# Expert stage of a Trainium2 kernel: token rows in blocks of 116 and 148 columns, the lower product turned round

## The reference, cut to what matters

```python
def moe_swiglu(t, w_router, w1, w3, w2):
    logits = (t @ w_router).astype(jnp.float32)
    top_v, top_i = lax.top_k(logits, TOP_K)                 # TOP_K = 2
    gates = jax.nn.softmax(top_v, axis=-1).astype(t.dtype)
    e_flat = top_i.reshape(-1)
    order = jnp.argsort(e_flat)
    tok = order // TOP_K
    xs = t[tok]
    sizes = jnp.bincount(e_flat, length=N_EXPERTS).astype(jnp.int32)
    h = jax.nn.silu(lax.ragged_dot(xs, w1, sizes)) * lax.ragged_dot(xs, w3, sizes)
    y = lax.ragged_dot(h, w2, sizes) * gates.reshape(-1)[order][:, None]
    return jnp.zeros_like(t).at[tok].add(y)
```

## Time and profile before

| | |
|---|---|
| median of 3 runs | 10121.22 us (10114.34 to 10128.42) |
| profiled execution: its time | 10121.75 us |
| profiled execution: its span | 10120.1 us |
| granted TensorE clock, mean | 0.969 |
| TensorE busy | 9577.1 us, 95% of the span |
| matmuls of the upper products, line 2387 | 3722.5 us busy, 32256 instructions |
| matmuls of the lower product, line 2397 | 1814.6 us busy, 4032 instructions |
| expert stage: its first DMA is issued at 4469.7 us, the next stage's at 10022.3 us | 5552.6 us |

### The profile page before, as it was taken

How to read it: one execution, slowest core, us unless ns; L and a number is a source line. 1 busy time by engine, 2 the same in 40 slices (tenths; PEclk the granted TensorE clock), 3 DMA queues, 4 the chain that set the end, 5 groups by cost and what they waited for, 6 DMA issues and landing times. The chain is left out here.

```text
span 10120.1 us, 132287 instructions
## 1 busy us (share of the span) xinstructions
PE 9577.1 (95%) x51446; PEld 6599.4 (65%) x51447; DVE 2676.1 (26%) x5608; ACT 1214.8 (12%) x3139; POOL 339.4 (3%) x524
## 2 busy tenths in 40 slices
PE   9974999999999998989999999999999999999995
PEld 3444577644444443458788788878788788788784
DVE  1137444332223224531111111111111111111113
ACT  1123233220000002220100100000100100100001
POOL 0010000012000000010000000000000000000002
PEclk9986999999999999989999999999999999999997
DMA  5312000149200002232211211122211211211224
GB/s 201 122 51 87 3 5 5 66 178 387 83 19 19 25 19 69 99 123 100 92 62 62 73 50 50 50 83 74 82 59 53 83 50 62 78 55 62 79 100 178
DMA packets 435311, 809.45 MB, mean 80 GB/s; under 512 B 24220, under 2 KB 304844, under 8 KB 428192
## 3 DMA queue, kind: packets, MB, share of 16 engines
q1 hardware_dynamic: 370598, 562.48, 16.2%
q0 software_dynamic: 59040, 224.13, 5.6%
q10 hardware_dynamic: 5472, 19.93, 0.6%
HBM read 573.91 MB, written 232.54 MB: 80 GB/s over the span
## 5 line engine op out<-in xcount | busy, mean ns | idle before, releaser
L2387 PEld LDWEIGHTS ex_psH<-ex_xt,ex_w 128*128 128x128 f32 x32256 | 3698.5, 193 | 381.0 <-issue 381.0
L2387 PE MATMUL ex_psH<-ex_xt,ex_w 128*128 x32256 | 3722.5, 277 | 100.7 <-issue 77.6
L2397 PE MATMUL ex_psY<-ex_w,ex_a 128*128 128x512 f32 x4032 | 1814.6, 593 | 6.1 <-DVE ex_a L2511 6.1
L2511 DVE TENSOR_TENSOR ex_a<-ex_s,ex_psH 128x128 f32<-128x128 f32 x1008 | 290.3, 288 | 4532.6 <-PE ex_psY L2397 3263.3
L550 PE MATMUL de_ps<-de_ht,de_w 128*128 128x512 f32 x2816 | 1222.9, 592 | 0.0
L2397 PEld LDWEIGHTS ex_psY<-ex_w,ex_a 128*128 128x128 f32 x4032 | 727.6, 191 | 730.6 <-issue 730.6
L550 PEld LDWEIGHTS de_ps<-de_ht,de_w 128*128 128x128 f32 x2816 | 535.1, 190 | 672.3 <-issue 672.3
L2476 ACT ACTIVATE ex_s<-ex_psH 128x128 f32<-128x128 f32 x1008 | 279.3, 277 | 5046.6 <-PE ex_psH L2387 5046.6
L566 PE MATMUL de_ps<-de_w,de_a 128*128 128x512 f32 x1408 | 621.9, 594 | 18.0 <-DVE hx_h L716 18.0
L2521 DVE TENSOR_TENSOR ex_ya<-ex_psY,ex_ya 128x512 f32 x936 | 603.1, 685 | 25.4 <-PE ex_psY L2397 25.4
L231 PE MATMUL en_psO<-en_w,en_ht 128*128 128x512 f32 (+1 forms) x1152 | 501.1, 592 | 2.0 <-ACT en_ht L273 2.0
(11 more groups left out here) (329 smaller groups left out, 4526.9 us busy)
## 6 DMA issues: line engine op xcount, KB each, us to landing
ex_w<-in_o_w SPq DMA_DIRECT2D x336, 1024.0 KB, 7.7
xs<-de_zero POOLq DMA_DIRECT2D x130, 512.0 KB, 32.9
ys<-de_zero POOLq DMA_DIRECT2D x130, 512.0 KB, 33.1
en_ch<-in_w_mod SPq DMA_DIRECT2D x48, 1024.0 KB, 5.0
de_w<-in_e_w SPq DMA_DIRECT2D x66, 512.0 KB, 5.8
ex_x<-xs ACTq DMA_DIRECT2D x38, 512.0 KB, 3.6
ys<-ex_ya POOLq DMA_DIRECT2D x36, 512.0 KB, 9.4
proj<-en_o POOLq DMA_DIRECT2D x18, 1008.0 KB, 4.1
```

What stands on the lines that cost most here:

```text
L2387: last = nc.tensor.matmul(psH[:, h, q * P:(q + 1) * P], W[:, s, k, h * P:(h + 1) * P], XT[:, k, bass.ds(at, P)], start=k == 0, stop=k == K ...
L2397: last = nc.tensor.matmul(psY[:, c], A[:, h], W2[:, s, h, c * BANK:(c + 1) * BANK], start=h == 0, stop=h == HU - 1)
L2511: nc.vector.tensor_tensor(A[:, h], S[:, h], psH[:, h, P:2 * P], ALU.mult).then_inc(a_done, 1)
```

## The change

The rows of an expert are cut into blocks of two widths, `SLIM` = 116 and `WIDE` = 148 columns. With N rows there are nt = max(2, ceil((N + 32) / 148)) blocks, of which ceil((N - 116 nt) / 32), at least one, are wide. `CT` now holds for each expert the slim and the wide blocks, their sum, the number of 128-row tiles that they touch, and the two running sums; `TI` is gone.

The lower product is turned round: a 128x128 piece of `W2` is the held weight, and the block's 116 or 148 columns of `A` move; its 8 output pieces lie in three PSUM banks (`PARTS`) and `YA` now holds results with the feature on the partition. A block is therefore 64 + 32 instructions of the block's width. `down` follows in the same block: three first products need only half 0 of `A`, then TensorE waits for half 1. The silu writes `A`, and VectorE multiplies in place. The `drain` stands at the end of each chunk.

Token rows are loaded by SP straight into `XT`, all tiles of an expert after the last W3 product of the expert before. Then each tile is turned in place: VectorE and ScalarE copy it into a fixed buffer `T` in four quarters, TensorE turns each quarter (2 transposes), and VectorE and ScalarE bring it back to `XT`. After the last chunk every tile of `YA` goes through `T` and back in the same way before POOL stores it. POOL clears `YA` once at the start.

```diff
+            N, MT, LEFT = (NX[:, q] for q in range(3))
             settle(nc.vector.scalar_tensor_tensor(N, IO[0:1, :], -float(SEQ), psA[0:1, 1, 0:NE], ALU.mult, ALU.add))
+            settle(nc.vector.tensor_tensor(MORE[:, :, :], N.rearrange("p (e j) -> p e j", j=1).to_broadcast([1, NE, STEPS]),
+                                           AT_LEAST[:, :, :].to_broadcast([1, NE, STEPS]), ALU.is_ge))
+            settle(nc.vector.tensor_reduce(MT, MORE[:, :, :], AXX, ALU.add))
+            settle(nc.vector.scalar_tensor_tensor(LEFT, MT, -float(SLIM), N, ALU.mult, ALU.add))
+            settle(nc.vector.tensor_scalar(NI[:, :], LEFT, float(STEP - 1 - 2 * SLIM), float(STEP), ALU.add, ALU.max))
+            nc.vector.tensor_scalar(LAY[:, 2], MT, 2.0, None, ALU.add)
+            settle(nc.vector.tensor_scalar(NI[:, :], NI[:, :], STEP.bit_length() - 1, None, ALU.logical_shift_right))
+            nc.vector.tensor_scalar(LEFT, LAY[:, 2], float(SLIM), float(P - 1), ALU.mult, ALU.add)
+            settle(nc.vector.tensor_scalar(LAY[:, 1], NI[:, :], 0.0, None, ALU.add))
+            nc.vector.tensor_tensor(LAY[:, 0], LAY[:, 2], LAY[:, 1], ALU.subtract)
+            settle(nc.vector.scalar_tensor_tensor(NI[:, :], LAY[:, 1], float(STEP), LEFT, ALU.mult, ALU.add))
             settle(nc.vector.tensor_scalar(NI[:, :], NI[:, :], 7, None, ALU.logical_shift_right))
+            nc.vector.memset(LAY[:, 4:6, 0:1], 0.0)
+            settle(nc.vector.tensor_scalar(LAY[:, 3], NI[:, :], 0.0, None, ALU.add))
             for e in range(1, NE):
+                settle(nc.vector.tensor_tensor(LAY[:, 4:6, e:e + 1], LAY[:, 4:6, e - 1:e], LAY[:, 2:4, e - 1:e], ALU.add))
+            nc.vector.tensor_copy(CT[:, :, :], LAY[:, :, :])
...
+MAXB = 64
+SLIM, WIDE, STEPS = 116, 148, 13
+STEP = WIDE - SLIM
...
+        A = m.sbuf("a", [P, HU, WIDE])
+        T = m.sbuf("t", [P, KD, P])
         psH = m.psum("psH", [P, HU, BANK])
+        psY = m.psum("psY", [P, 3, BANK])
+        psT = m.psum("psT", [P, 3, BANK])
+        turns = [psT[:, 0], psT[:, 1], psT[:, 2], psH[:, 1]]
...
+            def weights(e, i, s):
+                f = i * 2 + s
+                at = [bass.ds(v, 1) for v in (e, f)]
+                sp.wait_ge(w_used, e * FC + f + 1)
+                sp.sem_inc(passed_sp, 1)
+                sp.dma_start(W1[:, s], w1v[at[0], at[1]].rearrange("a b p k n -> p (a b k) n")).then_inc(w_in[s], 16)
+                sp.dma_start(W3[:, s], w3v[at[0], at[1]].rearrange("a b p k n -> p (a b k) n")).then_inc(w_in[s], 16)
+                sp.dma_start(W2[:, s], w2v[at[0], at[1]].rearrange("a b p h n -> p (a b h) n")).then_inc(w_in[s], 16)
+
+            def token_rows(e):
+                nd, t0 = count(sp, 3, e, 3, NT + 1), count(sp, 4, e, 0, MAXB)
+                sp.wait_ge(gate_done, t0 * (FC * HU) + 1)
+                sp.sem_inc(passed_sp, 1)
+                with sp.Fori(0, nd) as d:
+                    row = (d + e * NT).with_bounds(min_val=0, max_val=NE * NT)
+                    sp.dma_start(XT[:, :, bass.ds(d * P, P)], rows(xs_d, row).rearrange("p (k n) -> p k n", n=P)).then_inc(x_in, 16)
+
+            def rest(e):
+                weights(e, 0, 1)
+                with sp.Fori(1, FC // 2) as i:
                     for s in range(2):
+                        weights(e, i, s)
+
+            sp.dma_start(ident[:, :], ident_d).then_inc(const_in, 16)
+            sp.dma_start(mod[:, :, :], cols).then_inc(const_in, 16)
+            token_rows(0)
+            weights(0, 0, 0)
+            rest(0)
+            with sp.Fori(1, NE) as e:
+                weights(e, 0, 0)
+                token_rows(e)
+                rest(e)
...
+            pool.memset(YA[:, :, :], 0.0).then_inc(y_free, 1)
+            with pool.Fori(0, NE) as e:
+                nd, d0 = tiles(pool, e)
+                with pool.Fori(0, nd) as d:
+                    for q in range(NQ):
+                        pool.wait_ge(t_out[q], d0 * 2 + nd + d + 2)
+                    row = (e * NT + d).with_bounds(min_val=0, max_val=NE * NT)
+                    pool.dma_start(rows(ys_d, row).rearrange("p (k n) -> p k n", n=P), YA[:, :, bass.ds(d * P, P)]).then_inc(stored, 16)
+                pool.wait_ge(stored, (d0 + nd) * 16)
...
+            def experts_block(width, at, s, n):
+                for h in range(HU):
+                    for q, W in enumerate((W1, W3)):
+                        pe.wait_ge((s_done, a_done)[q], n * HU + h + 1)
+                        for k in range(KD):
+                            last = nc.tensor.matmul(psH[:, q, h * width:(h + 1) * width], W[:, s, k, h * P:(h + 1) * P],
+                                                    XT[:, k, bass.ds(at, width)], start=k == 0, stop=k == KD - 1)
+                        last.then_inc((up_done, gate_done)[q], 1)
+
+                def down(r, k, h):
+                    j = k - PARTS[r][0]
+                    return nc.tensor.matmul(psY[:, r, j * width:(j + 1) * width], W2[:, s, h, k * P:(k + 1) * P], A[:, h, 0:width],
+                                            start=h == 0, stop=h == HU - 1)
+                pe.wait_ge(a_done, n * HU + 2)
+                for r, (lo, hi) in enumerate(PARTS):
+                    pe.wait_ge(y_added, n * 3 + r + 1)
+                    down(r, lo, 0)
+                pe.wait_ge(a_done, n * HU + 3)
+                for r, (lo, hi) in enumerate(PARTS):
+                    down(r, lo, 1)
+                for r, (lo, hi) in enumerate(PARTS):
+                    for k in range(lo + 1, hi):
+                        for h in range(HU):
+                            last = down(r, k, h)
                     last.then_inc(y_done, 1)
...
+            def turn(n):
+                for q in range(NQ):
+                    pe.wait_ge(t_in[q], n + 1)
+                    pe.wait_ge(t_out[q], n + 1)
+                    for j in range(2):
+                        last = nc.tensor.transpose(turns[q][:, j * P:(j + 1) * P], T[:, 2 * q + j], ident[:, :])
+                    last.then_inc(t_done[q], 1)
...
+                with pe.Fori(0, nd) as d:
+                    turn(d0 * 2 + d)
+                for q in range(NQ):
+                    pe.wait_ge(t_out[q], d0 * 2 + nd + 1)
+                pe.sem_inc(passed_pe, 1)
+                with pe.Fori(0, FC // 2) as i:
+                    for s in range(2):
+                        lo = pe.snap(t0 * FC + (na + nb) * (i * 2 + s), min_val=0, max_val=MAXB * FC)
+                        pe.wait_ge(w_in[s], (e * (FC // 2) + i + 1) * 48)
+                        pe.sem_inc(passed_pe, 1)
+                        with pe.Fori(0, na) as j:
+                            experts_block(SLIM, pe.snap((j * SLIM).with_bounds(min_val=0, max_val=XW - SLIM)), s, lo + j)
+                        with pe.Fori(0, nb) as j:
+                            experts_block(WIDE, pe.snap((na * SLIM + j * WIDE).with_bounds(min_val=0, max_val=XW - WIDE)), s, lo + na + j)
                         nc.tensor.drain().then_inc(w_used, 1)
...
+                with pe.Fori(0, nd) as d:
+                    turn(d0 * 2 + nd + d)
...
+            def silu(width, n):
+                for h in range(HU):
+                    act.wait_ge(up_done, n * HU + h + 1)
+                    nc.scalar.activation(A[:, h, 0:width], psH[:, 0, h * width:(h + 1) * width], ACT.Silu).then_inc(s_done, 1)
+
+            def fill(src, at, n):
+                act.wait_ge(t_done[1], n + 1)
                 act.sem_inc(passed_act, 1)
+                nc.scalar.activation(T[:, 2:4], src[:, 2:4, bass.ds(at, P)], ACT.Copy).then_inc(t_in[1], 1)
...
+                    act.wait_ge(x_in, (d0 + nd) * 16)
+                    fill(XT, at, d0 * 2 + d)
+                    for q in (1, 3):
+                        act.wait_ge(t_done[q], d0 * 2 + d + 2)
+                        act.sem_inc(passed_act, 1)
+                        for j in range(2):
+                            k = 2 * q + j
+                            last = nc.scalar.activation(XT[:, k, bass.ds(at, P)], turns[q][:, j * P:(j + 1) * P], ACT.Identity,
+                                                        bias=mod[:, 0, k:k + 1], scale=mod[:, 1, k:k + 1])
+                        last.then_inc(t_out[q], 1)
...
+            def gather(width, at, n, fresh, e):
+                for h in range(HU):
+                    dve.wait_ge(s_done, n * HU + h + 2)
+                    dve.wait_ge(gate_done, n * HU + h + 2)
+                    nc.vector.tensor_tensor(A[:, h, 0:width], A[:, h, 0:width], psH[:, 1, h * width:(h + 1) * width], ALU.mult).then_inc(a_done, 1)
+                if fresh:
+                    dve.wait_ge(y_free, e + 1)
+                for r, (lo, hi) in enumerate(PARTS):
+                    dve.wait_ge(y_done, n * 3 + r + 1)
+                    out = YA[:, lo:hi, bass.ds(at, width)]
+                    y = psY[:, r, 0:(hi - lo) * width].rearrange("p (k n) -> p k n", n=width)
+                    if fresh:
```

(45 more changed lines are left out.)

260 lines of the change are left out of this document (79 added, 181 removed).

## The result

The changed kernel takes 10300.41 us (median of 4 runs, 10290.29 to 10306.15), the kernel before 10117.78 us beside it (10109.70 to 10128.42): ratio 1.018, interval 1.0168 to 1.0191. It is slower by 183 us; the forecast was 127 us slower. The profiled execution has a span of 10300.3 us and a mean granted TensorE clock of 0.959, for 0.969 before.

A forecast was written before the change was run, and what follows sets the result against it. The expert stage was taken as bound by TensorE's instructions times their pace, plus small gaps. Blocks -92, chunk ends +85, turning +188, between experts -52 and routing -2 gave +127 us on 10121.75: 10248 us, range 10120 to 10350.

The forecast's parts named there:

- end: After the last expert: 0.8 us for the last adds and 9 for the last store and barrier, 10 us.
- The blocks: Expert stage's products: slim steps 0.1117 us, wide 0.1259, so 5240 us for 5332, 92 us less.
- Rival 1: Slim block steps go by columns, 0.0993 us each, saving 298 us more: 9950 us; chance 0.07.
- The wait inside a block: TensorE's wait for half 1 of A is covered by 0.07 to 0.11 us; priced at nothing.
- Rival 4: The wait for half 1 of A shows by 0.2 us in 462 blocks, 92 us: 10340 us; chance 0.07.
- The chunk ends: Drain at each chunk's end exposes sequencer work, about 1.35 us, 104 times: 140 us for 55, 85 more.
- Rival 3: Inner loop's branch pays for its length, 48 x 3.8 = 182 us at chunk ends: 10430 us; chance 0.07.
- Turning: Tiles through T: XT 3.3 us, YA 2.8, 36 each way, 220 us where 32 go away: +188.
- Rival 2: Turning and chunk ends are cheap, at their low bounds: -17 us, 10104 us; chance 0.09.
- Between experts: Seven boundaries, 8.3 us each beside turning, 58 us; with start and end 81 for 133: -52.
- Start: First expert, beside turning: three tiles land at about 10.3 us, then 1.0 and 2.0: 13.3 us.
- The routing chain: Before the expert stage: nine dependent operations fewer, 1 to 3 us, taken as 2 us less.

The follow-up runs named there:

- run 4: Changed kernel with SLIM and WIDE at 132 and 164 instead of 116 and 148: 10080.24 us, ratio to the kernel before 0.9956.
- run 5: Changed kernel without the drain at chunk ends, SyncE waiting on y_done before reloading a weight slot: 10157.66 us, 143 us less.
- run 6: Kernel before the change with its drains removed, SyncE waiting on y_done instead: 10076.03 us, ratio 0.9960.
- run 1: Changed kernel with one Copy activation on a scratch column ahead of the loop that turns the XT tiles: 10263.04 us, 37 us less.

## Why the prediction was right or wrong

The direction, the mechanism and the range (10120 to 10350) held; the likeliest time, 10248, was 52 us low. Against the stage of 5731.3 us the steps miss by 40 (boundaries), 6 (block phases), some 7 (start) and -2 (end); the stage itself begins 2.3 us later, where 2 us earlier were forecast.

- **The blocks, -92: right.** Slim steps are 0.112 us, wide ones 0.126; with the chunk ends and eight starts at half clock 5240 + 140 + 16 = 5396 us were forecast, 5402.5 measured. Rival 1 (columns) is refuted by 128, 116, 100 and 64 columns at 7.31 us for 64 instructions, and by run 4, in which more columns are faster. What is shown is the pace; that the load of the weight sets it is argued, since no run has the same instructions without their loads.
- **The wait inside a block, nothing: right.** No idle time stands before the lower product. The step from the seventh to the eighth lower product of a slim block is 0.133 us for 0.112, 0.02 x 252 = 5 us. Rival 4 is out.
- **The chunk ends, 140 for 55: right.** 139 now, by run 5; of the 55 before, run 6 gave back 40 with longer waits at the boundaries. Rival 3 is out. These are the sequencer's branches of the inner loop (line 2443) and of the loop over experts (line 2435); the shortest of each are the loops' ends:

```profile
L2443 PEldq COMPARE_BRANCH  x56: 73/216/216, 4570.0 to 10187.8; - x56
...
L2435 PEldq COMPARE_BRANCH  x8: 83/214/214, 4996.4 to 10194.5; - x8
```

  The first, over 768 instructions, takes the 0.21 us of the old one over 576; with its register work it makes 0.56 us at 48 ends, 27 us, not 182. The second takes 0.21 us too, for 4.0 before, as the forecast took it. The Trainium skill's rule that rival 3 named ("Runtime: NRT & Kernel Launch", "Instruction fetch mechanics"), with pages of 256 instructions, would have put a stall at each branch back over 768 instructions; the 216 ns of that row disagree. The same section of the Trainium skill also gives TensorE room for 2048 instructions, and with that the 4.0 us over some 1800 disagree.
- **Turning, +188: the step that failed, in size.** The sentence "ScalarE's own chain: copy 0.4, wait 0.9, 1.5 us back, loop and semaphore counts 0.5: 3.3 us" left out the table load, 1.28 us a tile. The tiles of `XT` took 4.33 us in most steps and 4.17 on average; without the load (run 1) they take 2.95 and 3.08. So the load is worth 40 us at the boundaries (285.0 for 244.7), and run 1 as a whole gave back 37 us. The rest of the chain was put 0.2 us too high. The kernel before has 36 such loads of 1283 ns too, at its silu's line in the turning chunk, and no wait of TensorE there is put down to ScalarE. I had read that chain by its activations alone. Rival 2 fell with it.
- **Between experts, -52: 17 us too much.** The forecast has 44 us at the seven boundaries beside the tiles. Measured, 285 less 33 x 4.17 and 33 x 2.60 leaves 61: on average 1.6 us from the last lower product to the first copy (0.8 forecast), 5.2 for the counts (4.5) and 2.0 behind the last tile (1.0). That run 1's boundaries, 244.7 us, meet the 245 of the forecast is luck: without the load the tiles are 17 us below it and the rest 16 above.
- **Start.** The first upper product started 27.7 us after the stage's first DMA, for 13.3 - 2.0 + 3 x 3.3 = 21.2. Three tiles with the load make 3.1 of the difference, the rows' landing after 12.0 us for 10.3 another 1.7, and the clearing of `YA` 1.5: POOL's memset was priced at nothing, and beside VectorE it isn't. The routing chain gained nothing visible for the 2 us: the stage begins at 4472.0 us for 4469.7.

What the change was worth: the narrower blocks save 92 us of 5332 with 6.5% fewer columns, since 116 columns cost what 128 do, and the structure that allows free widths adds some 295 us (210 for turning, 85 for chunk ends) for some 30 back at the boundaries, the start and the end. The structure was not the loss: with a width above the load's pace, no drain, and turning that overlaps, the same structure is 2.9% faster than the kernel before, 2.5% faster than that kernel without its drains (9824.40 and 10076.03 us).

## What to carry to other kernels

Before you cut columns, find the pace that a matmul can't go below (here a row with 8 moved columns showed it) and choose the width so that no block lies under it: here 132 and 164 columns did in 30 blocks what 116 and 148 did in 33. A drain costs what can no longer run ahead behind it, so count that register work, or let the reader wait on a count that exists. When a chain is summed from durations, add the loads of function tables in it, and ask of each whether it stands in a loop or can stand ahead of it; here they stood in every pass of a loop in which no other table was wanted.

## What the runs showed of the hardware

- A matmul with its own load of a 128x128 float32 weight takes a step of 0.112 us for 8, 64, 100, 116 and 128 moved columns alike, at 2.4 GHz. At 1.2 GHz it is 0.215 us (64 columns).
- With 64 moved columns the granted clock fell to 0.62 over most of the first expert though TensorE was busy for 471 of 480 us; with 100 and 116 it was 1.00 in the same stretch. So cutting to 64 columns gained nothing and cost 900 us; the clock over an expert's blocks was between 0.64 and 0.95, and why it differs is open.
- VectorE's three copies of 256 columns took 3.21 us beside GpSimd's memset and 0.70 without; in four runs the first of them ended 0.14 to 0.15 us after the memset, whenever that was.
- A table load of ScalarE takes 1283 ns and can stand in each pass of a loop: 36 at the copy and 252 at the silu. One activation ahead of the loop made 8 of the 36 and gave back 37 us.
- Register work and drain of about 1 us and 0.56 us more with the loop's branch at a chunk's end were wholly hidden once no drain stood ahead.
